# Weight sums of a fast matrix product, moved from GpSimd to VectorE

## What is computed

```python
def swiglu(u, w_gate, w_up, w_down):
    return (jax.nn.silu(u @ w_gate) * (u @ w_up)) @ w_down

u = modulate(rmsnorm(h, g_ff1[l]), sh1, sc1)
h = h + FFN_RES * gt1[:, None, :] * swiglu(u, w1_gate[l], w1_up[l], w1_down[l])
...
u = modulate(rmsnorm(h, g_ff2[l]), sh3, sc3)
h = h + FFN_RES * gt3[:, None, :] * swiglu(u, w2_gate[l], w2_up[l], w2_down[l])
```

## Time and profile before

| | us |
|---|---|
| median of 3 runs | 1231.33 (1229.64 to 1231.72) |
| the profiled execution | 1231.31 |
| its span, first to last instruction | 1229.5 |
| mean granted TensorE clock | 0.986 of full |
| TensorE busy | 1195.8 (97%) |
| VectorE busy | 660.2 (54%) |
| ScalarE busy | 332.2 (27%) |
| GpSimd busy | 274.2 (22%) |
| chain of work that ended last: TensorE, VectorE | 90%, 6% of the span |
| DMA | 241.70 MB, 197 GB/s |

### The profile page before, as it was taken

One profiled execution on the slowest core, in us unless ns is written; L12 is line 12 of the kernel. 1 busy time (PEld: TensorE's weight loads), 2 busy tenths in 40 slices (PEclk: granted clock), 3 DMA queues, 4 the chain that ended last, 5 costly groups with the idle time before them and its releaser, 6 DMA issues.

```text
span 1229.5 us, 20015 instructions
## 1 busy us (share of the span) xinstructions
PE 1195.8 (97%) x8286; PEld 1075.1 (87%) x8286; DVE 660.2 (54%) x1512; ACT 332.2 (27%) x943; POOL 274.2 (22%) x169
## 2 busy tenths in 40 slices
PE   9998989999999999999799997999999999999997
PEld 7888989996688888889799997998888998888887
DVE  4457786372027533351689877557865323157632
ACT  2111210142124434100311210134324421146542
POOL 0008555100012000012356755340000310000101
PEclk9998999999999999999999998999999999999999
DMA  9969838582475555568399965848242563443321
GB/s 346 336 206 315 299 124 266 197 281 78 153 241 149 187 205 188 183 245 280 114 353 313 303 214 194 257 174 283 81 121 73 185 215 117 151 125 104 103 69 35
DMA packets 164139, 241.70 MB, mean 197 GB/s; under 512 B 13921, under 2 KB 112415, under 8 KB 164048
## 3 DMA queue, kind: packets, MB, share of 16 engines
q1 hardware_dynamic: 156160, 230.45, 55.5%
q10 hardware_dynamic: 6784, 5.74, 1.6%
q0 software_dynamic: 1104, 4.22, 1.0%
HBM read 236.82 MB, written 4.62 MB: 196 GB/s over the span
## 4 chain that ended last, share of the span: by engine, by line
PE 90%; DVE 6%; ACT 2%; POOL 1%; DMA 1%; issue 1%; DVEq 0%; ACTq 0%; POOLq 0%
PE ps L189 88%; PE ps L192 2%; DVE arena L198 2%; DVE tmps L204 1%; ACT U L195 1%; ACT tmps L195 1%; POOL arena L198 1%; DVE tmps L198 1%; DVE ABT L198 0%; DMA bias_row<-rows 0%; DMA arena<-bias_row 0%; DVE rstd L216 0%; DVE tmpA L198 0%; ACT arena L195 0%; DVE U L198 0%
## 5 line engine op out<-in xcount | busy, mean ns | idle before, releaser
L189 PE MATMUL ps<-U,slots 128*128 128x256 f32 (+2 forms) x2912 | 538.1, 344 | 0.2 <-DVE arena L198 0.2
L189 PEld LDWEIGHTS ps<-U,slots 128*128 128x128 f32 (+1 forms) x2912 | 465.5, 190 | 52.5 <-issue 5.0
L189 PE MATMUL ps<-arena,slots 128*128 128x128 f32 (+1 forms) x1840 | 272.6, 308 | 11.1 <-DVE arena L198 11.1
L189 PEld LDWEIGHTS ps<-arena,slots 128*128 128x128 f32 x1840 | 252.9, 192 | 27.9 <-DVE arena L198 11.4
L198 POOL TENSOR_TENSOR arena<-slots,arena 128x1024 f32<-128x1024 f32 (+1 forms) x44 | 132.9, 3021 | 125.4 <-DVE arena L198 89.7
L195 ACT ACTIVATE tmps<-ps 128x256 f32<-128x256 f32 (+2 forms) x151 | 57.4, 383 | 373.3 <-PE ps L189 361.4
L207 DVE CUSTOM_DVE_ANT_0 arena<-arena,tmpA 128x1024 f32<-128x1024 f32 x88 | 111.1, 1298 | 16.0 <-DMA arena<-in_w_adaT 15.5
L189 PE MATMUL ps<-arena 128*128 128x128 f32 (+7 forms) x940 | 106.7, 294 | 1.0 <-DVE arena L198 1.0
L189 PEld LDWEIGHTS ps<-arena 128*128 128x128 f32 (+2 forms) x940 | 97.4, 188 | 10.1 <-issue 4.3
L189 PE MATMUL ps<-ABT,arena 128*128 128x128 f32 (+5 forms) x752 | 86.6, 280 | 10.4 <-ACT tmps L195 6.7
L195 ACT ACTIVATE arena<-ps 128x512 f32<-128x512 f32 (+3 forms) x116 | 50.5, 459 | 153.4 <-PE ps L189 149.2
(11 more groups left out here) (181 smaller groups left out, 1097.6 us busy)
## 6 DMA issues: line engine op xcount, KB each, us to landing
slots<-in_w_in SPq DMA_DIRECT2D x14, 2048.0 KB, 9.4
slots<-in_w_down SPq DMA_DIRECT2D x16, 1408.0 KB, 7.9
slots<-in_w_gate SPq DMA_DIRECT2D x18, 1024.0 KB, 8.8
slots<-in_w_up SPq DMA_DIRECT2D x18, 1024.0 KB, 11.7
arena<-in_w_adaT SPq DMA_DIRECT2D x28, 512.0 KB, 5.5
slots<-in_w_adaT SPq DMA_DIRECT2D x7, 2048.0 KB, 8.4
arena<-in_ada_w1T SPq DMA_DIRECT2D x24, 512.0 KB, 9.2
slots<-in_a_in_w SPq DMA_DIRECT2D x6, 2048.0 KB, 10.3
```

The source lines that it names most:

```text
L189: return Nothing() if self.e is None else self.e.matmul(*a, **k)
```

## The change

- Gate/up blocks: `v_t1` becomes `v_t`, which forms t1, t2 and t3 on VectorE. GpSimd keeps t4 (`p_t4`), which now waits for VectorE's t2.
- Down pairs: all of t2, t3, t4 go to VectorE, t2 in `v_dn_t2`, t3 and t4 in `v_dn_t34`. GpSimd does nothing there.
- In `v_gu_blocks` all chunks of a round come after v_t of the next block (before: two of them ahead of t1). In round 10, t2 of pair 0 follows t1; its t3 and t4 come after the last v_sd.
- For pairs 1 and 2, t2, t3, t4 come between the chunks and `v_dn`.
- In f2, `v_su` moves ahead of the gates of block 0; before it stood behind their first halves and t1. In f1 it already stood ahead.
- In the diff, two hunks that repeat others for f2 are left out, and some of the semaphore lines of `t_gu` and `t_dn`.
- TensorE's order, ScalarE's order, the loads and all buffers stay; only the semaphores of t2, t3, t4 are VectorE's now.

```diff
-        def v_t1(e, f, b):
+        def v_t(e, f, b):
 
             t, free = TG.open(f, b)
             for x in free:
@@ -1056,15 +1056,15 @@
             e.wait_ge(*arrived(f + " gu", b))
             w = gu_block(f, b)
             e.tensor_tensor(t[:, 0], w[:, :, 0:4, P:T], w[:, :, 0:4, 0:P], ALU.subtract).then_inc(*dve.up(f, "t1", b))
...
-        def p_t(e, f, b):
+            e.wait_ge(*dve.at(f, "t1", b))
+            e.tensor_tensor(t[:, 1], w[:, :, 4:8, P:T], t[:, 0], ALU.subtract).then_inc(*dve.up(f, "t2", b))
+            e.tensor_tensor(w[:, :, 0:4, P:T], w[:, :, 4:8, P:T], w[:, :, 0:4, P:T], ALU.subtract).then_inc(*dve.up(f, "t3", b))
+
+        def p_t4(e, f, b):
 
             t, w = TG.buf(f, b), gu_block(f, b)
-            e.wait_ge(*dve.at(f, "t1", b))
             e.wait_ge(*arrived(f + " gu", b))
-            e.tensor_tensor(t[:, 1], w[:, :, 4:8, P:T], t[:, 0], ALU.subtract).then_inc(*pool.up(f, "t2", b))
-            e.tensor_tensor(w[:, :, 0:4, P:T], w[:, :, 4:8, P:T], w[:, :, 0:4, P:T], ALU.subtract).then_inc(*pool.up(f, "t3", b))
-            e.wait_ge(*pool.at(f, "t2", b))
+            e.wait_ge(*dve.at(f, "t2", b))
             e.tensor_tensor(t[:, 2], w[:, :, 4:8, 0:P], t[:, 1], ALU.subtract).then_inc(*pool.up(f, "t4", b))
...
             e.wait_ge(*dve.at("su", f))
-            e.wait_ge(*pool.at(f, "t2", b))
+            e.wait_ge(*dve.at(f, "t2", b))
             e.wait_ge(*act.at(f, "s1", b))
...
-            e.wait_ge(*pool.at(f, "t3", b))
+            e.wait_ge(*dve.at(f, "t3", b))
             e.wait_ge(*act.at(f, "u2", b))
...
-        def p_dn_t(e, f, p):
+        def v_dn_t2(e, f, p):
 
             lo, hi = dn_of(f, p)
-            t1, t2, t4 = (TD[(3 * p + n) % 4] for n in range(3))
+            t1, t2 = TD[3 * p % 4], TD[(3 * p + 1) % 4]
             e.wait_ge(*dve.at(f + " dn", "t1", p))
             e.wait_ge(*arrived(f + " dn", 2 * p + 1))
             if p:
                 e.wait_ge(*pe.at(f + " dn", "p5", p - 1))
-            e.tensor_tensor(t2, hi[:, :, P:T], t1, ALU.subtract).then_inc(*pool.up(f + " dn", "t2", p))
-            e.tensor_tensor(lo[:, :, P:T], hi[:, :, P:T], lo[:, :, P:T], ALU.subtract).then_inc(*pool.up(f + " dn", "t3", p))
+            e.tensor_tensor(t2, hi[:, :, P:T], t1, ALU.subtract).then_inc(*dve.up(f + " dn", "t2", p))
+
+        def v_dn_t34(e, f, p):
+
+            lo, hi = dn_of(f, p)
+            t2, t4 = (TD[(3 * p + n) % 4] for n in (1, 2))
+            e.tensor_tensor(lo[:, :, P:T], hi[:, :, P:T], lo[:, :, P:T], ALU.subtract).then_inc(*dve.up(f + " dn", "t3", p))
             e.wait_ge(*(pe.at(f + " dn", "p6", p - 1) if p else pe.at(f, "p4", 10)))
-            e.wait_ge(*pool.at(f + " dn", "t2", p))
-            e.tensor_tensor(t4, hi[:, :, 0:P], t2, ALU.subtract).then_inc(*pool.up(f + " dn", "t4", p))
+            e.wait_ge(*dve.at(f + " dn", "t2", p))
+            e.tensor_tensor(t4, hi[:, :, 0:P], t2, ALU.subtract).then_inc(*dve.up(f + " dn", "t4", p))
...
             e.wait_ge(*dve.at("sd", f))
-            e.wait_ge(*pool.at(n, "t2", p))
+            e.wait_ge(*dve.at(n, "t2", p))
             e.wait_ge(*act.at(n, "s1", p))
...
-            W.close([pe.now(), pool.at(n, "t4", p)], n, 2 * p + 1)
-            e.wait_ge(*pool.at(n, "t4", p))
+            W.close([pe.now(), dve.at(n, "t4", p)], n, 2 * p + 1)
+            e.wait_ge(*dve.at(n, "t4", p))
...
@@ -3258,17 +3263,17 @@
             for b in range(b0, 11):
                 if b > b0:
                     v_gu_act(e, f, b - 1)
-                chunks = CHUNKS[f].get(b, [])
-                v_ada_chunks(e, chunks[:2])
                 if b < 10:
-                    v_t1(e, f, b + 1)
+                    v_t(e, f, b + 1)
                 else:
                     v_sd(e, f, 0, 9)
                     v_dn_t1(e, f, 0)
-                v_ada_chunks(e, chunks[2:])
+                    v_dn_t2(e, f, 0)
+                v_ada_chunks(e, CHUNKS[f].get(b, []))
                 v_gu(e, f, b)
             v_gu_act(e, f, 10)
             v_sd(e, f, 9, 11)
+            v_dn_t34(e, f, 0)
...
             v_su(e, "f1", "n1")
             v_gate(e, "f1", 8)
-            v_t1(e, "f1", 5)
+            v_t(e, "f1", 5)
             v_gate(e, "f1", 9)
...
@@ -3306,6 +3311,9 @@
                 if p < 2:
                     v_dn_t1(e, "f1", p + 1)
                 v_ada_chunks(e, [(8 + p, c) for c in range(4)])
+                if p < 2:
+                    v_dn_t2(e, "f1", p + 1)
+                    v_dn_t34(e, "f1", p + 1)
                 if p == 1:
                     v_scale(e, "n2", V("g_mix"), 32)
                 v_dn(e, "f1", p, sm[:, 96:104], "n1")
...
+            v_su(e, "f2", "n3")
             v_gate(e, "f2", 0, 0)
             v_gate(e, "f2", 1, 0)
             e.wait_ge(*pe.at("sums", "n3", 1))
-            v_t1(e, "f2", 1)
-            v_su(e, "f2", "n3")
+            v_t(e, "f2", 1)
             v_gate(e, "f2", 0, 1)
             v_gate(e, "f2", 1, 1)
             v_silu_c2(e)
...
         def gpsimd(e):
             p_bias(e)
             for b in range(5, 11):
-                p_t(e, "f1", b)
-            for p in range(3):
-                p_dn_t(e, "f1", p)
+                p_t4(e, "f1", b)
...
             for b in range(1, 11):
-                p_t(e, "f2", b)
-            for p in range(3):
-                p_dn_t(e, "f2", p)
+                p_t4(e, "f2", b)
```

More of the change, by code:

```diff
@@ L1241, in t_dn @@
             product(C2[:, P:T], t1, SD[:, 0], False).then_inc(*pe.up(n, "p5", p))
-            e.wait_ge(*pool.at(n, "t3", p))
+            e.wait_ge(*dve.at(n, "t3", p))
             e.wait_ge(*act.at(n, "u2", p))
@@ L3395, in vector @@
                 v_ada_chunks(e, [(25 + p, c) for c in range(4)])
+                if p < 2:
+                    v_dn_t2(e, "f2", p + 1)
+                    v_dn_t34(e, "f2", p + 1)
                 if p == 1:
```

## The result

The changed kernel takes 1199.61 us in the median of four runs (1198.56 to 1201.15), the kernel before 1231.53 in the runs beside it: a ratio of 0.9745, 95% interval 0.9728 to 0.9762, 31.9 us less. 1201.7 was forecast.

A forecast was written before the change was run, and what follows sets the result against it. TensorE, 97% busy, was taken as the bound, so only pauses and slow-clock stretches could give time: 6.55 + 8.5 + 6.2 + 9.3 - 1.0 = 29.6 us off 1231.33, giving 1201.7; range 1198 to 1210.

The forecast's parts named there:

- f1 first block: f1's first seven-product block: p6 starts at 92.9, 4.0 us earlier, without the slow stretch, 2.56 more; gain 6.55 us.
- f1 down: f1's first down product: 6.0 us of pause and 2.47 of slow matmuls go; gain 8.5 us.
- f2 first block: f2's first seven-product block: p6 at 609.0 instead of 612.97, clock kept; gain 6.2 us, or 4.0 with clock lost.
- f2 down: f2's first down product: 6.8 us of pause and 2.5 of slow matmuls go; gain 9.3 us.
- f2 blocks: f2's blocks 2 to 8 may lose 0 to 0.45 us each, 0 to 3.2; a loss of 1.0 us taken.
- VectorE's round in f2: VectorE's loop per f2 block: 10.4 us without the t4 stall, 12.7 to 13.2 with it, against TensorE's 12.51.
- (A): Rival: VectorE sets the pace in f2, f1 joining above 13 us; 1204 to 1213 us, 25%.
- (B): Rival: the clock falls although pauses are short; 1204 us at f2's start, 1209 with the down products too; 9%.
- (C): Rival: weights arrive late on VectorE, needing a landing of 21 us against 11.7; 1233 us and more, 2%.
- (D): Rival: GpSimd doesn't cause VectorE's stretches, so VectorE stays slow and down products keep their pauses; 1224 us, 4%.
- The drain of the Trainium skill: VectorE's next operation waits for a drain: 0.95 us more per added sum, f2 loses about 15 us, 1216; 1%.
- The price paid elsewhere: f2's last gate matmuls wait for a PSUM buffer, 598.91 becomes 600.0, because v_su moves ahead; hidden.

The follow-up runs named there:

- three times t4: The changed kernel with GpSimd forming every gate/up t4 three times over, each needed only a block later: 1264.97 us, ratio 1.0282.
- the kernel with filled pauses: The kernel before with 22 extra matmuls, result unread, inside p2 of the first down product, before its last four records, both layers: 1226.89 us, ratio 0.9972.
- the run that held the ports: The changed kernel with GpSimd forming three more 128x1408 sums that nothing reads, after block 10's p4, in both layers: 1217.27 us, ratio 0.9897.

## Why the prediction was right, point by point

| step | forecast | measured in the profiled executions |
|---|---|---|
| f1 first block: delay and clock | 6.55 | p6 was 96.91 - 89.28 = 7.63 after p1, is 91.01 - 87.33 = 3.68; 6.30 - 3.77: 3.95 + 2.53 = 6.5 |
| f1 down | 8.5, p6 at +17.95 | p6 at 168.06 - 150.00 = +18.06; 5.94 + 2.37 = 8.3 |
| f2 first block | 6.2, with the clock kept | pause 6.65 became 1.38 + 1.30, p6 came 612.97 - 598.91 = 14.06 after the last gate's start, comes 592.03 - 583.32 = 8.71, and that gate is 1.17 later: 4.2; 5.98 - 3.81 = 2.2: 6.4 |
| f2 down | 9.3, p6 at +17.95 | 719.15 - 701.09 = +18.06; 6.70 + 2.42 = 9.1 |
| f2 blocks | -1.0 (0 to -3.2) | spacing (701.09 - 601.04) / 8 = 12.51: 0 |

The five come to 6.5 + 8.3 + 6.4 + 9.1 = 30.3 us, against 29.6 forecast, 31.9 in the medians and 29.8 when the changed kernel was measured again (1230.19 - 1200.37). The profiled executions differ by 32.8 us of span because they also began differently: the first p1 came at 87.33 instead of 89.28. That is no effect of the change. The difference is there at the first of f1's plain products, at 17.12 us instead of 19.07, before any weight sum; in the second profiled execution of the same changed kernel it came at 19.16, the first p1 at 89.38, and the span was 1199.0. Over all profiled executions here the first p1 came between 87.06 and 89.48, and both early and late ones are found with the old and with the new sums.

At f1's first block the cause is another than at the others. p6 waited for GpSimd's own first sum, which took 5.66 us; the change takes p6 off it, because VectorE has t1 to t3 done by 84.3, in its pause. That first GpSimd sum takes 5.67 us in the changed kernel too (as t4, from 89.25), and VectorE instructions with two SBUF operands run beside it unheld until 92.7. What GpSimd does in these first 3.4 us, no run here shows.

**The mis-sized term** is VectorE's round in f2: 12.7 to 13.2 us by the sum, 12.17 to 12.41 measured. Term by term, in the round from 631.98: activation 1.33 (1.4 in the sum), v_t 3.53 (3.6), stall 3.38 - 1.22 = 2.16 (2.34 to 2.80), chunks 3.66 (3.6), c1 and c22 1.02 (1.1), tanh 0.70. So most of the error is the stall: the sum took GpSimd's recorded lengths for it, while t4 ran against VectorE only from the end of t3 (635.71 + 1.22 = 636.93) to its own end (635.93 + 3.20 = 639.13), 2.2 us. The other terms come to 0.16 us less, the "some tenths less where starts overlap" that the forecast named and did not subtract. The late start was right to 0.3 (activation of block 1 at 607.24 - 601.04 = 6.2 into block 2, 6.5 by the sum). So the loss of 1.0 us didn't come.

**The rivals.** (A) was real as a mechanism and absent as a price: three times t4 turned it on. (B) did not happen in the changed kernel; the clock was 1.00 through the pauses of 1.38 and 1.30 us. That was partly luck, since the prediction's ground for it does not hold: in the kernel with filled pauses the clock fell after pauses of 0.99 and 1.00 us, so that pauses under 1.6 us keep it is no rule. (C) stood off: VectorE waited for no weights in the seven-product blocks. On the slower landing that it needs nothing was run. (D) fell with the run that held the ports. The drain of the Trainium skill ("VectorE: DVE Perf Modes", section "The DRAIN you can't avoid"), put on top of each sum, would have given a round of over 14 us, by the estimate in the prediction. The instructions of 1.22 us start 1.14 us apart, as before, so the trace disagrees with that reading.

**The price paid elsewhere** came as forecast: the gate's last matmuls wait 1.38 us for the PSUM buffer (1.1 forecast), hidden behind the c row.

## What to carry to other kernels

Before an engine is given work because it is idle, look at what it holds while it works: here a GpSimd sum of some 3 us cost VectorE 2.2 to 2.8 us when it ran whole against an instruction with two SBUF operands (1.1 at the c row, where it had partly run), and forming it there costs 1.14 to 1.6, so moving the sums to the busier engine made that engine sooner done at three of the four places; at the fourth it had a pause to form them in. Where the matmul engine is 97% busy, read the pauses one by one, ask for each what ended last, and add the slow matmuls behind it: 9.5 of the 30 us gained at the four places were clock, not waiting. A round of a loop on a second engine that comes to within a few tenths of the first engine's block time is worth adding up with start-to-start distances, not with recorded lengths.

## What the hardware showed that I had not expected

- The clock can fall after matmuls have resumed: in the filled f1 pause it was 1.00 up to 182.5 us, 0.66 in the next half us and 0.50 after that, so it fell about 1 us after a pause of 1.00 us had ended (181.7). Pauses of 0.88 and 1.00 in the same kernel's f2, and of 1.38 and 1.30 in the changed kernel's f2, left it alone. The length of the pauses alone doesn't tell.
- A waiting GpSimd got its turn after one VectorE instruction, even when VectorE had more queued: in the run with three t4, each of the three sums held one VectorE instruction of the round shown (646.49, 649.91 and 653.17: 3.38, 2.19 and 3.36 us), with at most one free chunk between them.
